# Scan of the two SSD layers: one broadcast of the running sums per head, with a ReLU on ScalarE and a select on GpSimd

## What is computed

```python
a_cum = jnp.cumsum(dA, axis=2)
seg = a_cum[:, :, :, None] - a_cum[:, :, None, :]
decay_ts = jnp.where(causal, jnp.exp(jnp.where(causal, seg, 0.0)), 0.0)
cb = jnp.einsum('bctgn,bcsgn->bctsg', C, B)
y_diag = jnp.einsum('bctsg,bctsgr,bcsgrp->bctgrp', cb, decay_ts, xdt)
```

## Time and profile before

| | |
|---|---|
| median of three runs | 1956.38 us (1956.15 to 1957.5) |
| the profiled execution | 1956.49 us, of which the span is 1954.9 us |
| TensorE busy | 1774.0 us, 91% of the span |
| VectorE busy | 1324.6 us, 68% |
| ScalarE busy | 950.4 us, 49% |
| GpSimd busy | 498.7 us, 26% |
| scan of layer 0 | about 180 to 227 us from the span's start |
| scan of layer 3 | about 1557 to 1604 us |

### The profile page before, as it was taken

The page is one execution under the profiler, slowest core; times in us unless marked ns, Lnnn a source line. Parts: engine busy times, 40 slices in busy tenths (PEclk is TensorE's granted clock), DMA queues, the critical chain, the costliest instruction groups (busy, mean ns, idle before and its releaser), DMA issues.

```text
span 1954.9 us, 35706 instructions
## 1 busy us (share of the span) xinstructions
PE 1774.0 (91%) x13457; PEld 1644.5 (84%) x13457; DVE 1324.6 (68%) x2471; ACT 950.4 (49%) x1722; POOL 498.7 (26%) x419
## 2 busy tenths in 40 slices
PE   6999989999999365899999959999999998999998
PEld 6998759999999233599999959999899875999997
DVE  5989795555575877465557876554799879565455
ACT  4456754453344755255435454533545666445333
POOL 1601401441120334154112015411160060044111
PEclk8999989999999667899999979999999998999999
DMA  6455474655547899765554517554545448465550
GB/s 211 142 181 152 141 230 133 201 183 183 172 169 233 314 398 410 266 207 186 173 172 135 170 55 234 178 183 161 157 139 184 125 137 265 130 200 177 183 175 26
DMA packets 317972, 365.05 MB, mean 187 GB/s; under 512 B 7802, under 2 KB 290978, under 8 KB 317750
## 3 DMA queue, kind: packets, MB, share of 16 engines
q1 hardware_dynamic: 296068, 287.41, 46.7%
q0 software_dynamic: 20560, 74.62, 10.1%
q10 hardware_dynamic: 1216, 1.35, 0.2%
HBM read 340.79 MB, written 23.15 MB: 186 GB/s over the span
## 4 chain that ended last, share of the span: by engine, by line
PE 66%; DVE 18%; ACT 7%; issue 3%; DVEq 3%; DMA 1%; POOLq 1%; POOL 0%; ACTq 0%; SPq 0%
PE G L551 19%; PE G L552 19%; PE G L553 19%; DVE wlo L1681 5%; ACT whi L1061 3%; DVE sums L1994 2%; PE A L997 1%; PE A L512 1%; DVE pg L2056 1%; DVE pg L2054 1%; DVE xbc L1842 1%; ACT raw L1247 1%; PE G L748 1%; DVEq L1844 1%; DVE stx L1986 1%
## 5 line engine op out<-in xcount | busy, mean ns | idle before, releaser
L1681 DVE TENSOR_TENSOR wlo<-raw,whi 128x2048 fp32r<-128x2048 f32 x234 | 547.7, 2341 | 335.8 <-ACT whi L1061 335.6
L1061 ACT ACTIVATE whi<-raw 128x2048 fp32r<-128x2048 f32 x234 | 448.0, 1914 | 560.0 <-PE G L553 555.8
L551 PE MATMUL G<-xH,whi 128*128 128x264 f32 x2112 | 605.0, 286 | 16.9 <-DVE wlo L1681 12.3
L552 PE MATMUL G<-xH,wlo 128*128 128x264 f32 x2112 | 600.1, 284 | 0.0
L553 PE MATMUL G<-xL,whi 128*128 128x264 f32 x2112 | 599.8, 284 | 0.0
L551 PEld LDWEIGHTS G<-xH,whi 128*128 128x128 f32 x2112 | 399.5, 189 | 26.8 <-DVE wlo L1681 13.5
L552 PEld LDWEIGHTS G<-xH,wlo 128*128 128x128 f32 x2112 | 399.7, 189 | 0.1
L553 PEld LDWEIGHTS G<-xL,whi 128*128 128x128 f32 x2112 | 397.8, 188 | 0.0
L551 PE MATMUL G<-aH,whi 128*128 128x264 f32 x1024 | 292.2, 285 | 7.9 <-DVE wlo L1681 7.9
L553 PE MATMUL G<-aL,whi 128*128 128x264 f32 x1024 | 290.7, 284 | 0.0
L552 PE MATMUL G<-aH,wlo 128*128 128x264 f32 x1024 | 290.7, 284 | 0.0
(11 more groups left out here) (440 smaller groups left out, 3032.2 us busy)
## 6 DMA issues: line engine op xcount, KB each, us to landing
raw<-in_mlp_w_up SPq DMA_DIRECT2D x64, 1024.0 KB, 5.3
raw<-in_mlp_w_down SPq DMA_DIRECT2D x64, 1024.0 KB, 5.1
raw<-in_ssd_w_in SPq DMA_DIRECT2D x48, 1024.0 KB, 5.4
pg<-in_cache_k POOLq DMA_DIRECT2D x64, 512.0 KB, 7.3
raw<-in_ssd_w_out SPq DMA_DIRECT2D x16, 1024.0 KB, 6.8
raw<-in_ple_w_gate SPq DMA_DIRECT2D x16, 1024.0 KB, 5.1
raw<-in_moba_w_qkv SPq DMA_DIRECT2D x12, 1024.0 KB, 5.2
pgw<-in_cache_v POOLq DMA_DIRECT2D x24, 512.0 KB, 7.4
```

Of the source, the lines that this page charges most:

```text
L551: mm(o, whi[u % 2][:, k, w], act_h[:, x, :], start=first, stop=False)
L552: mm(o, wlo[u % 2][:, k, w], act_h[:, x, :], start=False, stop=False)
L1061: fn(whi[u % 2][:], raw[(u + 2) % 4][:], ACT.Copy).then_inc(s_hi, 1)
L1681: V.tensor_tensor(wlo[u % 2][:], raw[(u + 2) % 4][:], whi[u % 2][:].bitcast(F32), ALU.subtract).then_inc(s_lo, 1)
```

## The change

The second broadcast (L626, L627) goes. ScalarE takes the second block from banks 4 and 5, whose columns 128 to 255 hold the unmasked running sums of the last 128 positions. It writes relu(a[s] - a[t]) into `seg` (per head, 128x128, ahead of the head's 128x256 Exp), with the running sum itself as the bias; `tm` gets a seventh block of columns for it. After the last head ScalarE waits for its own Exps and takes one Exp of all four heads, exp(-relu(a[s] - a[t])), 128x512, in place. This is exp(a[t] - a[s]) for t at or after s and 1 above the diagonal, so GpSimd then clears the entries above the diagonal (`cleared`, an affine select of 128x512), and VectorE's third product waits for that. The semaphore counts of `s_exp` go from three to two a group; `s_finT` at the end of the program is folded into `s_tp0`.

```diff
@@ ssd scan, TensorE, exponents(g)
                         if n:
-                            pe.wait_ge(s_exp, 3 * n - 2 + p)
+                            pe.wait_ge(s_exp, 2 * n - 1 + p)
...
-                    if n:
-                        pe.wait_ge(s_exp, 3 * n)
-                    for r in range(4):
-                        mm(bank[6][:, r * P:(r + 1) * P], sel(r), hv2["acHL"][:, P:SEQ], start=(r == 0), stop=False, skip_group_check=True)
-                    mm(bank[6].rearrange("p (r t) -> p r t", r=4), identB[:], past[:].unsqueeze(1).to_broadcast([P, 4, P]),
-                       start=False, stop=True, skip_group_check=True).then_inc(s_ar, 1)
...
-            final_T(3, G[last_bank], 1).then_inc(s_finT, 1)
+            final_T(3, G[last_bank], 1).then_inc(s_tp0, 1)
@@ ssd scan, ScalarE, decays(g)
                     for p in range(2):
-                        act.wait_ge(s_ar, 3 * n + p + 1)
+                        act.wait_ge(s_ar, 2 * n + p + 1)
                         for r in range(2):
-                            h = 4 * g + 2 * p + r
-                            f = fn(seg[:, 2 * p + r, 0:SEQ], bank[4 + p][:, r * SEQ:(r + 1) * SEQ], ACT.Exp, bias=hv2["tm"][:, 2, h:h + 1])
+                            h, row = 4 * g + 2 * p + r, bank[4 + p][:, r * SEQ:(r + 1) * SEQ]
+                            fn(seg[:, 2 * p + r, SEQ:3 * P], row[:, P:SEQ], ACT.Relu, bias=hv2["tm"][:, 6, h:h + 1], scale=-1.0)
+                            f = fn(seg[:, 2 * p + r, 0:SEQ], row, ACT.Exp, bias=hv2["tm"][:, 2, h:h + 1])
                         f.then_inc(s_exp, 1)
-                    act.wait_ge(s_ar, 3 * n + 3)
-                    for r in range(4):
-                        h = 4 * g + r
-                        f = fn(seg[:, r, SEQ:3 * P], bank[6][:, r * P:(r + 1) * P], ACT.Exp, bias=hv2["tm"][:, 3, h:h + 1])
-                    f.then_inc(s_exp, 1)
+                    act.wait_ge(s_exp, 2 * n + 2)
+                    later = seg[:, :, SEQ:3 * P]
+                    fn(later, later, ACT.Exp, scale=-1.0).then_inc(s_later, 1)
@@ ssd scan, GpSimd
+                def cleared(g):
+
+                    n = GROUPS * q + g
+                    pool.wait_ge(s_later, n + 1)
+                    later = grp[f"seg{g % 2}"][:, :, SEQ:3 * P]
+                    gp.affine_select(out=later, in_=later, compare_op=ALU.is_ge, fill=0.0, base=0,
+                                     pattern=[[0, 4], [1, P]], channel_multiplier=-1).then_inc(s_sel, 1)
                 for g in range(GROUPS):
                     scaled(g)
+                    cleared(g)
                     if 1 <= g < 7:
                         build(g - 1)
@@ z stage, VectorE, columns()
+                    V.tensor_copy(tm[:, 6:7], tmp[:, 3:4])
@@ ssd scan, VectorE, masked(g)
-                        dve.wait_ge(s_exp, 3 * n + p + 1)
+                        dve.wait_ge(s_exp, 2 * n + p + 1)
...
-                    dve.wait_ge(s_exp, 3 * n + 3)
+                    dve.wait_ge(s_sel, n + 1)
                     w = seg[:, :, SEQ:3 * P]
                     V.tensor_tensor(w, w, bc(bank[2][:, SEQ:3 * P], 4), ALU.mult).then_inc(s_M, 1)
```

More of the change, by code:

```diff
@@ L182, in build_trunk @@
             S[f"T{b}"] = at(f"T{b}", [P, 2, 268], o5 + 2144 * b)
-        hv2, _ = row(x1, [("rawlast", [P, CT, LAST]), ("hv", [P, XT, 17]), ("tm", [P, 6, HEADS]), ("ys", [P, XT, NB]),
+        hv2, _ = row(x1, [("rawlast", [P, CT, LAST]), ("hv", [P, XT, 17]), ("tm", [P, 7, HEADS]), ("ys", [P, XT, NB]),
                           ("acHL", [P, SEQ], F32R), ("id2", [P, HEADS], F32R), ("grs", [GROUPS, SEQ]),
@@ L269, in build_trunk @@
         s_gq = sem("s_gq")
+        s_sel, s_later = sem("s_sel"), sem("s_later")
         s_dt7 = sem("s_dt7")
@@ L278, in build_trunk @@
                                                  sem("s_pje"), sem("s_tg"))
-        s_fin, s_finT, s_finE = sem("s_fin"), sem("s_finT"), sem("s_finE")
+        s_fin, s_finE = sem("s_fin"), sem("s_finE")
         s_mtp, s_msc, s_mex, s_mP = sem("s_mtp"), sem("s_msc"), sem("s_mex"), sem("s_mP")
@@ L685, in ssd @@
                     else:
-                        pe.wait_ge(s_exp, 3 * GROUPS * (q + 1))
+                        pe.wait_ge(s_exp, 2 * GROUPS * (q + 1))
                         for k in range(GROUPS):
@@ L1457, in _ @@
             act.wait_ge(s_fin, 5)
-            act.wait_ge(s_finT, 1)
+            act.wait_ge(s_tp0, 4)
             fn(fin["yrow"][:, 0, :], G[last_bank - 1][:].rearrange("p a b -> p (a b)"), ACT.Copy, scale=rstd[:, 0:1])
@@ L2367, in _ @@
             dve.drain().then_inc(s_fin, 1)
-            dve.wait_ge(s_finT, 1)
+            dve.wait_ge(s_tp0, 4)
             V.tensor_scalar(fin["yrow"][:, 1, :], G[last_bank][:].rearrange("p a b -> p (a b)"), rstd[:, 1:2], None, ALU.mult).then_inc(s_finE, 1)
```

## The result

The changed kernel takes **1963.51 us** (1962.14 to 1968.31), the kernel before on the same chip 1957.45 (1955.35 to 1960.66): a ratio of 1.0033, 95% interval [1.0022, 1.0044]. So it is slower, by 6.1 us between the medians: 0.33%, small, but clear of the noise. The forecast was 1958.2, which is 1.8 over before and within 0.2%.

What follows compares the result with a forecast made beforehand. TensorE was taken to pace groups 4 to 7 of the scans, then loops through the select; 0.89 us later in each of two layers, +1.8 on 1956.4, gave 1958.2 us, range 1954 to 1963.5.

Steps and rivals of the forecast that it cites:

- The prices: Assumed lengths of the scan's new ScalarE and GpSimd work; first Relu to later Exp's end 3.20 us, before 2.6.
- a = 0.65: Assumed length in us of GpSimd's new 128x512 affine select, with bounds 0.28 to 1.13.
- Loop A: One-group cycle in the scan: third product, GpSimd's xde, select, next third product; 4.80 us.
- loop B: Two-group cycle in the scan through VectorE, TensorE's `back`, ScalarE and the select; 10.19 us against 10.49 before.
- TensorE will wait in every group: Claim for the scans: TensorE idles about 0.5 us a group ahead of `back`, ended by L1960.
- The walk: Layer 0's third products followed group by group; group 7 ends 0.89 us late, layer 3 likewise, +1.8 us in all.
- the sentence on the removal: Removed TensorE work, 0.71 us a group or 11.4 in all, counts only where TensorE is late, not in groups 0-3.
- The clock: Rival, chance 0.03: waiting TensorE is granted 0.84 of full speed; four groups, two layers, +2.4 us more.
- The range up to 1963.5: Upper bound: select at 1.13 us gives +5.6, ScalarE's own wait at 0.3 us gives +1.5.
- TensorE's pace: Rival, chance 0.09: four TensorE-paced groups in each of two scans shed 0.71 us each, 5.7 in all; 1950.7.
- one-input price: Select priced near 0.61 us by width; the rival two-input price, 1.04 us, chance 0.22, meant +4.9, 1961.3.
- The select never met VectorE's split: Answers a rival, chance 0.04: select slowed beside VectorE's split to 1.35 us, +7.4 in all, 1963.8.

Runs made afterwards that it cites:

- the second profile: The changed kernel measured and profiled again without any edit: 1961.44 us against 1956.43 for the kernel before, ratio 1.0028.
- all kept: The changed kernel with the removed broadcasts and mask product put back, unread, in every group: 1961.03 us, ratio 1.0015 to the kernel before.

## Why the prediction was wrong

**The prices held.** Select 0.634 (a = 0.65 taken); Relu's slot 0.25 to 0.27 (0.25); a pair 0.62 or less (0.61); ScalarE's wait for itself 0.03 (0.05); later Exp 0.63 (0.61); first Relu to the end of the later Exp 3.26 (3.20). Relu brought no table load in the scans.

**The two loops held.** Loop A was to be 4.80 and is 4.73 to 4.74; loop B 10.19 and is 10.14 (203.41 to 213.56 is 10.15, 208.82 to 218.96 is 10.14). GpSimd is who VectorE waits for. TensorE's wait ahead of `back`, ended by the gate (L1963), was expected at 0.5 in every group; it is 0.74 in every second one, 0.37 in the mean, so "TensorE will wait in every group" was wrong.

**The walk held.** Start of the third product behind the scan's first `xd`, so that the 1.34 us by which this execution was later beforehand drop out, as delay against before. Three starts of before that the rows do not show, groups 1, 4 and 6:

```profile
189.60 0.68 DVE L1950 TENSOR_TENSOR seg<-seg,A 128x512 f32<-128x512 f32 x1
...
205.89 0.68 DVE L1950 TENSOR_TENSOR seg<-seg,A 128x512 f32<-128x512 f32 x1
...
216.40 0.68 DVE L1950 TENSOR_TENSOR seg<-seg,A 128x512 f32<-128x512 f32 x1
```

In the changed kernel groups 0, 1 and 7 start at 188.04, 191.22 and 223.71; the others are above.

| group | 0 | 1 | 2 | 4 | 6 | 7 |
|---|---|---|---|---|---|---|
| predicted, us late | 0 | 0.43 | 0.38 | 1.65 | 1.33 | 0.89 |
| measured, layer 0 | 0 | 0.28 | 0.37 | 1.59 | 1.23 | 0.72 |

The state copy is 0.73 late, as the third product of group 7: the delay passes on whole. Two undisturbed scans would make +1.5, against the +1.8 of the forecast. With the products of group 0 or of groups 0 and 1 kept the times lie 1.17 and 1.22 over before: that is the forecast, met by kernels that differ from the changed one by products that nobody reads.

**What failed is the clock, in two steps.** The first is the sentence on the removal: "only where TensorE is late; in groups 0 to 3 it waits for others", so worth nothing there. In the queues that is right: the products kept in groups 0 and 1 add nothing to a scan (43.92 to 43.98 with them, 43.93 without). But at the scan's start TensorE waits anyway, 1.34 us at one place without the products and 0.72 with them, and with this filling gone its granted clock falls. The second is the rival named "The clock": it was given a chance of 0.03, was placed in groups 4 to 7 at a mean of 0.84, and priced at +2.4 in all. The range up to 1963.5 was made of the select's price and ScalarE's wait alone and had no term for the clock. Measured: it falls at group 0, for 6.8 us and in five scans 3.4 more, in 9 scans of 12. With both stretches, as in each fall of the changed kernel, it costs some 3.6 us in a scan (47.51 against 43.93; 47.71 and 47.50 in the second profile); with the first alone 1.6 to 2.2 (43.77 against 42.20, 44.43 against 42.75, 47.05 and 46.81 against 44.82 with all kept). The row it rested on, 0.84 in 220 to 290, belonged to the stage behind the scan (before, the scan itself has 1.00 to its end); the place to look was the start of the scan, where TensorE waits in the kernel before as well and the removed products covered part of the wait.

The sum with this term: 2 x 0.75 for the queues and, for the changed kernel's three profiles, 4 falls in 6 scans, 2 x 4/6 x 3.6 = 4.8; together 6.3 us. Between the medians lie 6.1 in the first measurement and 5.0 in the second. The share of falls comes from six scans, so 4.8 is a rough figure; the 3.6 of one fall (3.5 to 3.8 in four) is not.

**The other rivals.** TensorE's pace did not decide, as the loops said. The select kept its one-input price: by the row, 0.634 at 512 columns against 0.282 at 128 is 0.92 ns a column, near the 0.86 of the memsets. The Trainium skill, GPSIMD Engine Reference, Engine selection, says the same (one-input work at about line rate), and the run agrees. The select never met VectorE's split: in group 2, where the split runs, the select waits for ScalarE until 198.01, and the split is over by 196.91. One reading under that rival was off: "xde beside such work" at 214.07 ran beside almost nothing, as VectorE idled from 213.99 until 215.19:

```profile
215.19 1.28 DVE L1947 TENSOR_TENSOR seg<-seg,A 128x512 f32<-128x512 f32 x2 [1.20 <-ACT seg L1220]
```

The row that shows the point is the next one, `bdL` at 215.21, which took its usual 1.90 beside this product.

**What stays open** is why the chip lets a given scan fall and another not. Layer 0 of the first profile had the same products missing and nearly the same wait of TensorE at its start as layer 3 (1.30 against 1.34), and stayed at 2.4 GHz:

```profile
184.80 0.44 PE L513 MATMUL A<-ident,xq 128*128 128x128 f32 x2 [1.30 <-DVEq L1933]
```

Nor does any run tell why layer 3 fell each time and layer 0 only half the time. That the fall hangs on the products of groups 0 and 1 is shown by 16 scans against 12. That those of group 0 suffice rests on two scans of one profile, one of them in layer 3, where all six scans without them fell; and in the falls seen the clock drops 0.9 to 1.9 us behind the scan's start, ahead of the place of group 1's products (2.1 us behind it, as L626 at 1562.27 before, with the scan's start at 1560.17).

## What to carry to other kernels

Ahead of taking work off TensorE, look for the places where it already waits, and ask what fills the time there: at such a place the removed work may be what keeps the granted clock up, and without it the products that follow take twice as long until the clock is back. Read the granted clock of the very stage and its neighbours in time, not a mean over a longer stretch. If a removal makes a stage longer with the same queues, put the work back unread at one place at a time: that tells the clock from the queues in a few runs. Take more than one profile: layer 0's scan of the changed kernel fell in one of three.

## What the runs showed beside it

GpSimd slowed down beside VectorE's split in a new place. Group 2 of the changed kernel, layer 0; GpSimd's two `xde` products, and the split on VectorE:

```profile
194.15 3.23 POOL L1553 TENSOR_TENSOR xde<-xd,tm 128x256 f32<-128x256 f32 x2 [1.10 <-DVE xd L1941]
198.01 0.64 POOL L1573 TENSOR_SCALAR_AFFINE_SELECT seg<-seg 128x512 f32<-128x512 f32 x1 [0.63 <-ACT seg L1220]
```

```profile
194.55 2.36 DVE L1683 TENSOR_TENSOR wlo<-raw,whi 128x2048 fp32r<-128x2048 f32 x1 [0.48 <-ACT whi L1056]
```

The pair took 3.23 us where it takes 1.18 elsewhere. Before, it was `xmL` that met the split and took 3.95 where 1.90 is usual, beside a split of 2.65; the split is 2.36 now, against 2.29 alone. Two different operations lost the same 2.05 us beside a split, so the loss goes with the neighbour and not with the operation; VectorE loses little. The Trainium skill, GPSIMD Engine Reference, Specifications, puts such contention down to VectorE's instructions with two SBUF inputs, which the split has. Here it delayed nothing, since the select behind it waits for ScalarE anyway.
